# The order of scores and values inside an attention slot of TensorE

## The reference

```
o_c: softmax(q . kc) vc      # kc, vc: 63 compressed blocks            "cmp"
o_s: softmax(q . ks) vs      # causal, over the selected blocks         "slc"
o_w: softmax(q . kw) vw      # causal, the last 512 keys                "win"
o = gt[..., 0:1] * o_c + gt[..., 1:2] * o_s + gt[..., 2:3] * o_w
```

## Time and profile before

| | us |
|---|---|
| median of 3 runs | 2165.35 |
| lowest and highest | 2164.25, 2174.62 |
| the profiled execution, its own time | 2164.23 |
| its span in the trace | 2162.5 |
| PE busy | 2068.1 |
| DVE busy | 1194.7 |
| ACT busy | 759.8 |
| attention of the two groups | about 137 to 309, and 403 to 575 |

### The profile page before, as it was taken

The page is one execution under the profiler, slowest core; times in us unless marked ns, Lnnn a source line. Parts: engine busy times, 40 slices in busy tenths (PEclk is TensorE's granted clock), DMA queues, the critical chain, the costliest instruction groups (busy, mean ns, idle before and its releaser), DMA issues.

```text
span 2162.5 us, 26969 instructions
## 1 busy us (share of the span) xinstructions
PE 2068.1 (96%) x9802; PEld 1669.3 (77%) x9802; DVE 1194.7 (55%) x1855; ACT 759.8 (35%) x1203; POOL 252.8 (12%) x210
## 2 busy tenths in 40 slices
PE   5979989799899999999999999999999999999998
PEld 4956659466588888888788888887788888888887
DVE  6547756477422233233623442535977777777777
ACT  4346654566422111121311232323333333333232
POOL 1002340023200000000000000003511111111110
PEclk9989999799899999999999999999999999999999
DMA  6010000000011111121112111321121212211112
GB/s 171 1 39 1 1 16 1 0 1 1 16 52 52 52 49 39 48 76 30 36 45 67 44 44 44 101 99 40 49 59 40 57 48 58 58 44 53 48 58 88
DMA packets 148697, 98.87 MB, mean 46 GB/s; under 512 B 22203, under 2 KB 140173, under 8 KB 148621
## 3 DMA queue, kind: packets, MB, share of 16 engines
q1 hardware_dynamic: 148621, 97.85, 16.0%
HBM read 93.64 MB, written 4.19 MB: 45 GB/s over the span
## 4 chain that ended last, share of the span: by engine, by line
PE 91%; DVE 5%; ACT 2%; issue 1%; POOL 1%; DMA 0%; SPq 0%; ACTq 0%; DVEq 0%; POOLq 0%; PEldq 0%
PE bank L1945 11%; PE bank L1947 11%; PE bank L1946 11%; PE bank L2098 11%; PE bank L2106 6%; PE bank L2107 6%; PE bank L2108 6%; PE bank L2047 4%; PE bank L1847 2%; PE bank L1869 2%; PE bank L1874 2%; PE bank L1890 1%; PE bank L1870 1%; PE bank L1892 1%; PE bank L1891 1%; PE bank L1791 1%
## 5 line engine op out<-in xcount | busy, mean ns | idle before, releaser
L1945 PE MATMUL bank<-actT_h,ring_h 128*128 128x512 f32 x832 | 325.4, 391 | 3.5 <-DVE ring_l L1355 3.5
L1946 PE MATMUL bank<-actT_l,ring_h 128*128 128x512 f32 x832 | 324.7, 390 | 0.0
L1947 PE MATMUL bank<-actT_h,ring_l 128*128 128x512 f32 x832 | 324.7, 390 | 0.0
L1355 DVE TENSOR_TENSOR ring_l<-raw,ring_h 128x1024 fp32r<-128x1024 f32 x84 | 102.7, 1223 | 339.8 <-ACT ring_h L896 339.6
L1622 DVE TENSOR_TENSOR x<-x,bank 128x1024 f32<-128x1024 f32 x176 | 212.5, 1217 | 39.1 <-PE bank L2098 38.7
L1945 PEld LDWEIGHTS bank<-actT_h,ring_h 128*128 128x128 f32 x832 | 156.9, 189 | 36.6 <-issue 3.9
L1947 PEld LDWEIGHTS bank<-actT_h,ring_l 128*128 128x128 f32 x832 | 156.8, 189 | 32.9
L1946 PEld LDWEIGHTS bank<-actT_l,ring_h 128*128 128x128 f32 x832 | 156.9, 189 | 32.4
L896 ACT ACTIVATE ring_h<-raw 128x1024 fp32r<-128x1024 f32 x84 | 88.6, 1055 | 125.8 <-PE bank L1947 123.2
L866 ACT ACTIVATE pT<-bank 128x512 f32<-128x512 f32 (+1 forms) x148 | 88.1, 596 | 115.7 <-PE bank L1874 109.4
L1315 DVE TENSOR_REDUCE nmx<-bank 128x1 f32<-128x512 f32 (+4 forms) x154 | 95.4, 639 | 59.4 <-PE bank L1849 48.5
(11 more groups left out here) (330 smaller groups left out, 4211.6 us busy)
## 6 DMA issues: line engine op xcount, KB each, us to landing
raw<-in_w_in SPq DMA_DIRECT2D x60, 512.0 KB, 3.8
raw<-in_w_up SPq DMA_DIRECT2D x44, 512.0 KB, 5.0
wd_raw<-in_w_down SPq DMA_DIRECT2D x22, 512.0 KB, 3.6
raw<-in_w_branch SPq DMA_DIRECT2D x32, 256.0 KB, 2.8
x_in<-in_x SPq DMA_DIRECT2D x8, 512.0 KB, 8.1
raw<-in_w_o SPq DMA_DIRECT2D x8, 512.0 KB, 3.7
x<-in_x SPq DMA_DIRECT2D x8, 512.0 KB, 9.0
out<-x SPq DMA_DIRECT2D x8, 512.0 KB, 2.6
```

What stands on the lines that cost most here:

```text
L1355: nc.vector.tensor_tensor(dst, src, hi.bitcast(F32), ALU.subtract).then_inc(pl_done, 1)
L1945: nc.tensor.matmul(o, wh(k), ah[:, k, cols], start=k == 0, stop=False)
L1946: nc.tensor.matmul(o, wh(k), al[:, k, cols], start=False, stop=False)
L1947: ins = nc.tensor.matmul(o, wl(k), ah[:, k, cols], start=False, stop=k == k_tiles - 1)
```

## The change

In each slot the values of unit u - 3 are issued before the scores of unit u. Nothing else is moved: rows stay first, turn and final last. The programs of ACT, DVE, POOL and SP are the same row by row.

```diff
                     for piece in slot["pieces"]:
                         rows(*piece)
+                    if slot["values"]:
+                        values(*slot["values"])
                     if slot["unit"]:
                         scores(*slot["unit"])
-                    if slot["values"]:
-                        values(*slot["values"])
                     if slot["turn"] is not None:
```

## The result

The changed kernel takes 2173.7 us in the median of 20 runs (2169.5 to 2176.4), the kernel before 2165.2 us in the same number (2163.3 to 2174.9). The ratio is 1.003 with a 95% interval of 1.0019 to 1.0041: slower by 4 to 9 us, within the 0.5% that I had named. The profiled execution has a span of 2173.2 us.

The account below looks back on a forecast made before the run. PE was taken as the engine waited for in nearly every slot. Terms of +7.5, -4.4 and +0.4 sum to +3.5 us on the profiled 2164.23, so 2167.7; the forecast was 2168.0 us, range 2160 to 2176.

Parts of the forecast that it names:

- my own case: The whole kernel takes 2165 to 2171 us; given 52 in 100.
- the second rival: Weight loads behind masks and turns bring nothing, as values pay there what scores paid: 2172.1 us; 17 in 100.
- Turns behind the scores: Gaps from ACT's copy oT to PE's turn shrink by 0.70 us, so turns wait: 3.7 us a group, +7.5 both.
- Weights behind a short matmul: Behind a mask, turn or final, values' shorter weight load saves 0.06 us at 37 places a group: -4.4 us.
- The start: Slots 5 to 10: scores of unit 5 end later, the exponential starts 0.25 us late, through to L1825: +0.4 us both groups.
- The end: The group's last listed turn, gap 0.43 us, loses 0.38 us a group, counted within the turns' +7.5.
- My own formula: Each turn loses 0.11 - (gap - 0.70) us where positive, gap being from copy oT's end to the turn's start before.
- the waits don't come: Rival: values done earlier might make the copy oT earlier, so only the loads count: 2160.2 us; 2 in 10.
- the loads bring nothing: The second rival: the first values matmul might pay behind a mask what scores pay now; 2172.1 us, 17 in 100.
- the waits grow from slot to slot: Rival: held turns delay scores, exponential and next copy; 2188 us if all 40 turns pay 0.70 us; 8 in 100.

Follow-up runs that it names:

- copy_first: The changed kernel with ACT's copy oT moved ahead of the exponential in the copy's slot; median 2165.2 us, ratio to before 0.9981.
- before_copy_twice: The kernel before, order untouched, with a second copy of the same bank ahead of each copy oT on ACT; ratio to before 1.0022.
- before_turn_later: The kernel before with the turn, sum and final of each task one slot later; a single run, 2176.9 us.
- copy_first_late: As copy_first, but values go ahead of scores only from slot 10 on; median 2161.9 us, ratio to the kernel before 0.9968.

## Why the prediction held, and where it was off

The forecast was 2168.0 us and the median 2173.7. That lies in the range of 2160 to 2176, but outside my own case of 2165 to 2171; it is nearest to the 2172.1 of the second rival, whose mechanism did not come about. So the mechanism held, and the time fell in the range with help from that rival's room. The sum was +3.5 us and attention measured +7.0 in the profiles. By its terms:

- *Turns behind the scores, +7.5.* Right in kind, place and size. I read the 19 turns of the middle in the changed kernel's timeline, first group: the distance from the last scores matmul to the turn, less 0.23, sums to 4.5 us. But 1.1 of that is no wait: copy_first, in which no turn of the middle is held, still has it, 0.19 us in five of these slots (turns 11, 12, 13, 17, 18), whose scores are masked so that their last matmul starts early, and 0.06 in two more. That leaves 3.45 a group against 3.35 of my 3.73 (the last 0.38 lies in the end), and the middle of copy_first, in which finals wait 0.5 us as here, says 3.67. Turns 17 and 9 lost more than I had put (0.23 and 0.70, for 0 and 0.66), those behind the values of a cmp unit about 0.1 less.
- *Weights behind a short matmul, -4.4.* The middle of copy_first, without the turns' waits, is 1.21 us shorter than before, 1.91 with the 0.70: -3.8 us for both groups. The Trainium skill's rule (TensorE: Matmul & The Clock Gate, LDWEIGHTS: columns divided by 1.2 ns) had given 3.9 as an estimate. That the two are so near is partly luck, for more is in it than the term. By the trace there are 39 places a group from slot 11 on and not 37, 35 of them in the middle; at the 37 places of the first group in which values of 128 rows follow a mask (slots 11 to 70) the second matmul starts 0.30 or 0.31 us after it, as forecast. Two things that I had missed go the other way. Behind the last values of a cmp unit, whose weights are 64 rows and not 128, the next matmul starts 0.32 us later in place of 0.23. Before, the turn came there, with 0.27 us to the matmul behind it; now the scores do, and their second matmul starts 0.66 us after those values, where 0.46 is usual: 0.06 lost at each of 6 places. And at two places the values behind a mask are those of a cmp unit, whose second matmul starts 0.45 us after the mask and not 0.30. Against that, finals wait 0.5 us in the middle of copy_first and 0.9 before. All of this was read, not tested.
- *The start, +0.4.* The stretch measured +0.6, but that is the clock and not the term. The scores of unit 1 already start 0.49 and 0.26 us later after the group's first scores than before, and no values stand in the program up to there (the first come in slot 3). From the first scores to those of unit 1, changed kernel first (columns as above):

```profile
138.90:143.68 4.78, 4.78 (x23) 3.32 (x24) 0.32 (x1) 1.23 (x2) 0.00 (x0) 0.51 0.00 0
```

```profile
138.01:142.30 4.29, 4.29 (x24) 3.12 (x24) 0.13 (x1) 1.23 (x2) 0.00 (x0) 0.58 0.00 0
```

  Each group begins at half speed, for 4.7 and 4.6 us in the changed kernel and 3.6 and 4.1 before. From unit 1 to the values of unit 12 it is 38.58 us now and 39.36 before, so with the 0.70 the change itself made the start 0.08 shorter. The term was right where I had placed it: the chain from the exponential of unit 5 to L1825 came 0.7 and 0.5 us late, which less the 0.49 and 0.26 is 0.21 or 0.23 (L1825 waited 1.5 us, not 1.9). From slot 11 on the shorter loads took that back: the scores of slots 11, 12 and 13 start 1.37, 1.32 and 1.26 us later than before.
- *The end, within the turns as 2 x 0.38.* This is the term that was mis-sized: +2.8 us. The turn of task 20, whose gap of 0.43 us was the last of my list, lost 0.69 us a group and not 0.38, because more than 0.70 was taken from between: from the last scores matmul to the values of unit 71 it is 1.48 us before and 0.50 now. The values that stood in between are those of a cmp unit, which take 0.84 us up to the turn and not 0.70, and the scores ahead of them had an exposed step too (0.37 us, now 0.28). My own formula with 0.98 in place of 0.70 gives 0.66. The other part I had put at nothing: PE's clock fell to half speed while the group's last values were under way (at 307.4 us, 168.6 after the first scores; before at 170.9), which cost 0.8 and 0.6 us. Why it fell there is open.

With the measured sizes the order makes 7.3 - 3.8 - 0.2 + 1.4 = 4.7 us, and half-speed clock at the start and the end of the groups 0.7 + 1.5 = 2.2: together 6.9, against 7.0.

The rival that the waits don't come fell with the new wait in the profile. That the loads bring nothing fell with the 0.30 us behind the masks and with copy_first. The one that the waits grow from slot to slot didn't come about: the middle of before_copy_twice and that of the changed kernel both agree with losses that are simply added up.

What is still open is the clock. In the profiled executions a half-speed stretch of 3 to 7 us, twice, stood right behind PE's waits of slots 8 to 11 in some groups and not in others, and where they lasted 6.8 and 3.4 us they cost 3.0 to 3.1 us a group, counted from the scores of unit 1 and against a group without them and with the same order in these slots. In copy_first at its first group, and before (columns as above):

```profile
160.00:165.00 5.00, 3.65 (x11) 1.93 (x12) 3.23 (x12) 3.86 (x8) 0.00 (x0) 0.73 0.00 0
165.00:175.00 10.00, 9.31 (x31) 5.78 (x32) 6.40 (x13) 2.57 (x5) 1.04 (x1) 0.67 0.01 2
```

```profile
160.00:165.00 5.00, 3.69 (x16) 2.29 (x17) 3.61 (x13) 4.08 (x8) 0.00 (x0) 1.00 0.01 2
165.00:175.00 10.00, 9.08 (x45) 5.45 (x45) 7.91 (x17) 3.12 (x6) 2.40 (x2) 1.00 0.01 2
```

I first took the order of slots 5 to 9 for the cause. It isn't: the stretches are absent in both groups of the changed kernel, which has the new order there, and present in the second group of before_copy_twice and before_turn_later, which have the old one. So of copy_first_late's lead over copy_first, about 3 us a group, nothing is shown to be its edit's; its lead over the kernel before is measured, and 1.2 us a group of it are the middle's.

## What to carry to other kernels

When work is moved ahead on the busiest engine, list who hangs on what it was moved past: here ACT's copy hung on the scores by its place in ACT's program, not by a semaphore. For each such pair the gap read in the timeline, less the length of what was taken from between, gives the loss, and in the middle of these groups the losses added up. The length has to be read for each pair: 0.70 us was right for nearly all, and 0.98 for the last. An order on one engine pays only together with the order on the engine that feeds it back: values first alone costs 7 us of attention (2.2 of them at half-speed clock), the early copy alone brings nothing, and the two together have a middle 1.2 us a group shorter than before. The first and last slots of a pipeline are costed apart, since there the neighbours that cover a move are missing. And a stretch that begins or ends at half speed is compared only after the clock's part has been taken out, which a stretch that the change doesn't touch can show.

## What the hardware showed that I had not expected

The granted clock can fall to half at places where PE has waited for a few microseconds, and the same program point can have it or not: among the 24 groups profiled, 9 had such a stretch in slots 9 to 13. At the end of a group the stretch began between 167 and 175 us after the first scores; whether that was before or after the last values decided whether 0.8 us were lost. Without such a stretch the time repeats closely: from the scores of unit 1 to the values of unit 12 the six groups with the old order and no stretch took 39.36 to 39.38 us.

DVE's low part (L1307) took 741 ns in the mean after the change and 699 before, with the same operands. The growth lies in those that run beside an operation of POOL: 62 of them with a mean of 816 ns, where before 70 had 716; the 86 that have no POOL operation beside them took 687 ns, as before (683). copy_first has 743 ns too, with a middle shorter than before, so DVE had slack for it. Why the same overlap costs more now I did not find out.
